# A decoder trunk on one core: picks of expert heads moved beside the next unit, and an inverse root that scales the last tanh

## The chip, the cores and the metric

One core of one Trainium2 chip. The metric is the device time of the whole program in microseconds (us), the median of three runs. Engines: TensorE (PE; PEld is its weight load), VectorE (DVE), ScalarE (ACT), GpSimd (POOL), SyncE (SP, which here only issues DMAs).

## The reference, cut to what matters

One inference step of a two-layer trunk for 256 prompt tokens and 64 sample tokens, width 1024, all float32. Layer 0: a Mamba-2 mixer, then a PEER channel mixer, then a per-layer embedding. Layer 1: dilated attention over shared keys and values (the samples also over 2048 cached ones), then PEER and embedding again. PEER and embedding:

```python
def peer(u, w_query, sub_keys, expert_u, expert_v):       # per token
    q = (u @ w_query).reshape(8 heads, 2, 128)
    s = einsum('thcd,ckd->thck', q, sub_keys)             # 128 scores, two per head
    top_s, top_i = top_k(s, 16)
    cand = top_s[..0.., :, None] + top_s[..1.., None, :]  # 16 x 16
    best_s, best_j = top_k(cand, 16)                      # 16 of 16384 experts per head
    gate = softmax(best_s)
    act = gelu(einsum('td,thkd->thk', u, expert_u[idx]))
    return einsum('thk,thkd->td', gate * act, expert_v[idx])

h = h + peer(rmsnorm(h, norm_ffn), ...)
g = sigmoid(rmsnorm(h, norm_ple) @ ple_w_gate)
h = h + (p @ ple_w_proj) * g
```

## The kernel before, in words

**Units and phases.** Tokens lie in three tiles t: two of 128 prompt tokens, one of 64 sample tokens. After the Mamba mixer (up to about 559 us) the work goes by six units (layer, tile): (0,0), (0,1), (0,2), (1,0), (1,1), (1,2). A unit needs 128 blocks of rows of expert_u and as many of expert_v (64 for tile 2). A block is one indirect DMA that POOL issues (line 2446): 128 rows of 4 KB, 0.52 MB. Phase ph mixes the "u" blocks of unit ph with the "v" blocks of unit ph-1 (`phase_blocks`, six u first). Rows go to a ring of 14 slots, in one order for all engines. DVE takes a u block: the dot with u (`dot`, line 2114), which frees the slot. PE takes a v block: the weighted sum into PSUM banks 6 and 7 (`combine`, line 1070), which frees its slot. POOL waits for the slot's last user, and at u blocks 0, 32, 64 and 96 for the pick of that quad (`expert`).

**What runs beside them.** Each engine's program holds a generator of steps beside the blocks (`beside(ph)`). `due(ph, i)` spreads its SIDE_STEPS evenly over the blocks of the phase. Phases 0 and 1 do the picks of layer 0. Phase 2 runs `chain(0)`, phase 3 `chain(1)`, phase 4 `chain(2)`, phases 5 and 6 the embedding of layer 1 for tiles 0 and 1. A chain has these steps: the embedding of layer 0 (11), keys and values (11), q (6 of 14), rotary embedding (`normalise_heads`), attention, output projection, a norm, and last `ask(t)`: the query projection of layer 1 (16 steps, 8 MB of weights), its scores, and the picks. `pick_quad` (DVE, 5 steps, from line 1967) finds for two heads, a quad of four score rows, the 16 best of 128 twice, then of 256, and the experts' numbers. For t = 0 and 1 `ask` has 29 steps; DVE waits 7, then picks four quads in 20 steps, then ends the softmax (`finish_select`, 2 steps). Phase 2 has 89 steps on 192 blocks, phase 3 has 96 on 192, phase 4 has 105 on 256.

**Scores.** ACT copies the scores of quad q to `sc[:, q % 2]` (`take_score`); for q of 2 and 3 it first waits for the pick of quad q-2.

**Between phases.** DVE ends the side steps, takes the sums of the unit before to h (`take_peer`) and copies the next u to PSUM (`show_u`, line 2137). From then on it can do dots of the new phase.

**SP.** Weights come through a ring of four slots of 1 MB (`load_weights`, line 267). In phase 3 SP loads the mask of the samples (line 1295, `masks[:, 768:2480]`) once the prompt's attention ends. In phase 4, when the q projections have ended, it issues the cached keys and values (lines 1283, 1285, 1287), and behind them the new heads' store (`store_heads`, line 1273). `sample_max(0)` on DVE (line 2249) waits for that store and for the masks.

**The tail.** After the last v block: `take_peer(1, 2)`, the norm of 64 rows x 1024 (square on ACT, 15 small DVE operations for the inverse root, scaling at line 1833), eight turns on PE, two copies on ACT, the gate's matmuls (line 1167), the projection (1173), tanh (1803), four DVE operations (2372, 2374, 2377), one store (1251).

Of the kernel before, what the change touches and what calls it, by code (L numbers as in the profile page):

```python
# [17 lines left out]
D = 1024  # L18
# [112 lines left out]
def build(nc, I, O, counts):  # L131
# [3 lines left out]
    with ctx:  # L135
# [236 lines left out]
        def chain_steps(t):  # L372
            return 5 + 6 + 5 + 6 + 14 + (14, 21, 38)[t] + 2 + 3 + 5 + (29, 29, 21)[t]
# [72 lines left out]
        angles = small[:, 1136:1184].rearrange("p (t c f) -> p t c f", t=3, c=2)  # L446

# [83 lines left out]
        def _(pe):  # L531
# [294 lines left out]
            def ask(t):  # L826
# [5 lines left out]
                for i in range(27 if t < 2 else 0):  # L832
# [298 lines left out]
            def beside(ph):  # L1131
# [5 lines left out]
                elif ph == 1:  # L1137
                    yield from second_select
                    yield from select(0, 2)
                elif ph < 5:  # L1140
                    yield from chain(ph - 2)
                else:
                    yield from embed(1, ph - 5)

# [15 lines left out]
            pe.wait_ge(*prow_in.at((1, 2)))  # L1160
            transposes(("pT", 1, 2), [(c * 128, p_rows[0:64, c * 128:(c + 1) * 128]) for c in range(2)])
            norm_transposes("ple1", (2,))
            pe.wait_ge(*freed(("pT", 1, 2)))
            gate = claim(pe, ("last_gate",))
            for k in range(KD):
# [4 lines left out]
            proj = claim(pe, ("last_proj",))  # L1170
            for k in range(2):
                for n in range(2):
                    mm = pe.matmul(proj[64 * n:64 * n + 64, :], pT[:, k, 0:64], proj_w[:, k, n * 512:(n + 1) * 512],
                                   start=(k == 0), stop=(k == 1))
            mm.then_inc(*full(("last_proj",)))
# [3 lines left out]
        def _(sp):  # L1179
# [68 lines left out]
            def store_tokens(t):  # L1248
                sp.wait_ge(*dve_done.at(("ple", 1, 1, t)))
                dst = O["y_prompt"][0, OFF[t]:OFF[t] + 128, :] if t < 2 else O["y_sample"].rearrange("b s d -> (b s) d")  # L1250
                sp.dma_start(dst, h[0:ROWS[t], t, :]).then_inc(stored.sem, 16)
# [39 lines left out]
            for t in range(3):  # L1291
                load_ple_rows(0, t, (0, t - 1) if t else None)
                if t == 2:
                    sp.wait_ge(*full_at(("oT", 1)))
                    sp.dma_start(masks[:, 768:768 + SCOLS], I["masks"][:, 1152:]).then_inc(*masks_in.mark("S", 16))
# [48 lines left out]
            sp.wait_ge(stored.sem, 144)  # L1344
# [6 lines left out]
        def _(act):  # L1351
# [81 lines left out]
            def take_score(l, t, q):  # L1433

                bank = filled(act, ("score", l, t, q))
                if q >= 2:
                    act.wait_ge(*dve_done.at(("gate_in", l, t, q - 2)))
                elif (l, t) != (0, 0):
                    l0, t0 = UNITS[3 * l + t - 1]
                    act.wait_ge(*dve_done.at(("gate_in", l0, t0, HPT[t0] // 2 - 1)))  # L1440
                freeing(act.activation(sc[:, q % 2, :, :], bank.rearrange("p (j r) -> p j r", j=4), ACT.Copy), ("score", l, t, q))  # L1441
# [94 lines left out]
            def ask(t):  # L1536
# [5 lines left out]
                for i in range(27 if t < 2 else 0):  # L1542
                    if 1 <= i <= 16:
                        take_query(t, i - 1)
                    if i in (6, 10, 14, 18):
                        take_score(1, t, (i - 6) // 4)
                    yield
# [221 lines left out]
            def beside(ph):  # L1769
# [5 lines left out]
                elif ph == 1:  # L1775
                    yield from second_select
                    yield from select(0, 2)
                elif ph < 5:
# [703 lines left out]
```

## Time and profile before

| | us |
|---|---|
| median of 3 runs | 2655.35 (2652.01 to 2661.92) |
| the profiled execution | 2655.78 |
| its span | 2653.9 |
| PE busy | 1841.1 (69%) |
| DVE busy | 1580.7 (60%) |
| POOL busy | 1329.1 (50%) |
| ACT busy | 301.0 (11%) |

The span runs from the first instruction to the last; the execution's own time has 1.9 us more around it. All rows come from this execution. L12 is line 12 of the kernel before; a name such as `arena<-peer_u` is what an instruction writes and reads. "Idle before" is the time in which the engine did nothing ahead of the instruction, and behind the arrow stands what ended it. A window (A:B, us from the span's start) gives its length, then busy us and the count of instructions for PE, PEld, DVE, ACT and POOL, then the granted TensorE clock (1.00 is full), the DMA engines' busy share and GB/s; where it is asked of one line, only the engines that run it are listed. A group of lines gives the count, busy us, mean ns of one, and idle us before it. A timeline gives start and length in us, the engine (SPq: SP's queue), line and instruction, and idle us in brackets.

### The profile page before, as it was taken

The numbers are of one execution on the slowest core, as the hardware profiler recorded it, in microseconds if no ns is written. First come the engines' busy times: TensorE is split into PE (matmuls) and PEld (weight loads), VectorE is DVE, ScalarE is ACT, GpSimd is POOL, SyncE is SP. The second block draws the span as 40 slices with busy tenths as digits, with TensorE's granted clock in tenths as the row PEclk, the third lists the DMA queues.
The fourth block names the chain that finished last, engine by engine and source line by source line (L and its number), as shares of the span: only waits on it lengthen the run. The fifth ranks groups of instructions, "written<-read, shape, count | busy, mean of one in ns | idle before, by whom it ended". The sixth has DMA issues, their size and how long they took to land. (4 is left out here: it accounts for less than half of the span.)

```text
span 2653.9 us, 23578 instructions
## 1 busy us (share of the span) xinstructions
PE 1841.1 (69%) x7672; PEld 817.0 (31%) x7672; DVE 1580.7 (60%) x3814; ACT 301.0 (11%) x698; POOL 1329.1 (50%) x1480
## 2 busy tenths in 40 slices
PE   7999789776605666678687667755765658566677
PEld 4477656632600010022342224431123422001112
DVE  2288854779798756652659739797454433833311
ACT  2133312100100000010110102100012100000000
POOL 0011432244646777754755446645554443577772
PEclk9999879887856665689888787876877868699999
DMA  4231227469999999999999999998999989999995
GB/s 149 96 127 64 85 88 235 148 252 382 401 339 345 409 409 409 409 399 384 390 403 405 352 371 362 405 402 302 397 395 348 335 316 381 386 409 409 409 408 231
DMA packets 325768, 859.13 MB, mean 324 GB/s; under 512 B 26825, under 2 KB 93337, under 8 KB 325617
## 3 DMA queue, kind: packets, MB, share of 16 engines
q0 software_dynamic: 184320, 671.17, 64.7%
q1 hardware_dynamic: 141326, 186.46, 20.3%
q8 instruction: 62, 1.02, 0.2%
q14 instruction: 60, 0.49, 0.1%
HBM read 845.25 MB, written 12.17 MB: 323 GB/s over the span
## 5 line engine op out<-in xcount | busy, mean ns | idle before, releaser
L2114 DVE SCALAR_TENSOR_TENSOR arena<-arena,banks 128x1024 f32<-128x1024 f32 x640 | 763.2, 1219 | 476.9 <-DMA arena<-peer_u,arena 471.1
L1070 PE MATMUL banks<-arena 128*32 128x512 f32 x2560 | 707.5, 727 | 340.2 <-DMA arena<-peer_v,arena 329.7
L2446 POOL DMA_INDIRECT arena<-peer_v,arena x640 | 610.3, 954 | 437.4 <-issue 202.4
L2446 POOL DMA_INDIRECT arena<-peer_u,arena x640 | 607.6, 949 | 418.6 <-issue 186.2
L1070 PEld LDWEIGHTS banks<-arena 128*32 128x32 f32 x2560 | 92.8, 117 | 829.8 <-DMA arena<-peer_v,arena 680.6
L863 PE MATMUL banks<-wring,uT 128*128 128x512 f32 (+3 forms) x448 | 224.2, 649 | 60.2 <-DMA wring<-w_q 31.5
L537 PE MATMUL banks<-cst,arena 128*128 128x128 f32 (+5 forms) x514 | 79.9, 305 | 182.7 <-DVE arena L2130 84.9
L863 PEld LDWEIGHTS banks<-wring,uT 128*128 128x128 f32 (+1 forms) x448 | 80.2, 189 | 210.1 <-issue 164.4
L606 PE MATMUL banks<-uT,wring 128*128 128x320 f32 x512 | 139.1, 433 | 0.0
L537 PEld LDWEIGHTS banks<-cst,arena 128*128 128x128 f32 (+5 forms) x514 | 63.1, 156 | 233.9 <-DVE arena L2130 86.7
L565 PE MATMUL banks<-wring,uT 128*128 128x512 f32 (+1 forms) x256 | 116.5, 612 | 0.0
L606 PEld LDWEIGHTS banks<-uT,wring 128*128 128x128 f32 x512 | 96.7, 190 | 40.2 <-issue 0.8
L2393 POOL COPY arena<-arena 128x3 f32<-128x3 f32 x32 | 6.0, 186 | 186.8 <-ACT arena L1407 186.8
L537 PE MATMUL banks<-cst,u 128*128 128x128 f32 (+1 forms) x244 | 40.3, 324 | 77.6 <-DVE u L1833 73.2
L807 PE MATMUL banks<-uT,wring 128*128 128x128 f32 x512 | 70.7, 297 | 14.1 <-issue 14.1
L1956 DVE MAX8 arena<-arena 128x8 f32<-128x128 f32 (+1 forms) x240 | 68.3, 326 | 16.7 <-ACT arena L1441 15.8
L807 PEld LDWEIGHTS banks<-uT,wring 128*128 128x128 f32 x512 | 65.2, 207 | 36.7 <-issue 36.7
L1959 DVE FIND_INDEX8 arena<-arena 128x8 uint32<-128x128 f32 (+1 forms) x240 | 76.1, 329 | 0.0
L1098 PE MATMUL banks<-wring,uT 128*64 128x512 f32 (+1 forms) x128 | 63.3, 649 | 13.0 <-DMA wring<-ssm_w_out 11.9
L2165 DVE TENSOR_SCALAR arena<-arena 128x512 f32<-128x512 f32 (+1 forms) x10 | 4.2, 425 | 111.4 <-ACT arena L1573 111.4
L2425 POOL TENSOR_TENSOR arena<-arena,small 128x1024 f32<-128x1024 f32 x10 | 19.3, 1930 | 96.9 <-PE banks L537 96.6
L565 PEld LDWEIGHTS banks<-wring,uT 128*128 128x128 f32 (+1 forms) x256 | 45.2, 182 | 69.0 <-issue 68.9
(249 smaller groups left out, 1988.6 us busy)
## 6 DMA issues: line engine op xcount, KB each, us to landing
wring<-peer_w_query SPq DMA_DIRECT2D x40, 1024.0 KB, 18.9
wring<-ssm_w_in SPq DMA_DIRECT2D x24, 1024.0 KB, 7.5
wring<-w_q SPq DMA_DIRECT2D x18, 1024.0 KB, 21.9
wring<-ssm_w_out SPq DMA_DIRECT2D x16, 1024.0 KB, 9.6
wring<-ple_w_gate SPq DMA_DIRECT2D x12, 1024.0 KB, 12.6
arena<-peer_u,arena POOLq DMA_INDIRECT x640, 11.7
arena<-peer_v,arena POOLq DMA_INDIRECT x640, 12.2
out_sample_ssm<-arena SPq DMA_DIRECT2D x16, 512.0 KB, 5.4
```

The lines of the kernel that those rows point to most:

```text
L537: mm = pe.transpose(bank[0:c, col:col + r], src, ident[0:r, 0:r])
L565: mm = pe.matmul(acc[t][0:ROWS[t], 0:w.shape[2]], uT[:, kk, OFF[t]:OFF[t] + ROWS[t]], w[:, k, :], start=(kk == 0), stop=(kk == kchunks - 1))
L606: mm = pe.matmul(acc[:, 0:NTOK], w[k // 4][:, k % 4, j * 128:(j + 1) * 128], uT[:, k, :], start=(k == 0), stop=(k == KD - 1))
L807: mm = pe.matmul(bank[:, 0:R], w[k // 4][:, k % 4, (b % 4) * 128:(b % 4 + 1) * 128], uT[:, k, OFF[t]:OFF[t] + R], start=(k == 0), stop=(k ...
L863: mm = pe.matmul(bank[0:ROWS[t], 0:w.shape[2]], uT[:, kk, OFF[t]:OFF[t] + ROWS[t]], w[:, k, :], start=(kk == 0), stop=(kk == kchunks - 1))
L1070: mm = pe.matmul(sums(t, at, half), place_of(t, at), rows_buf[:, k, half * 512:(half + 1) * 512], start=at < spots(t), stop=False, skip_gr ...
L1098: mm = pe.matmul(acc[t][0:ROWS[t], :], uT[:, kk, OFF[t]:OFF[t] + ROWS[t]], w[:, k, :], start=(kk == 0), stop=(kk == 15))
L1956: step(j, dve.max(out_v[:, o], values))
L1959: step(j, dve.max_index(out_i[:, o], out_v[:, o], values))
L2114: dve.scalar_tensor_tensor(rows_buf[:, k, :], rows_buf[:, k, :], 1.0, u_now, ALU.mult, ALU.mult, accum_out=pact[:, n % 2, at:at + 1]).then ...
L2425: s(pool.tensor_tensor(hh, hh, spread(ec[:, blk, :], 128), ALU.mult), pool_done, ("h0s", blk))
L2446: pool.indirect_dma_start(rows_buf[:, k, :], None, tables[kind], bass.IndirectOffsetOnAxis(ap=rows, axis=0))\
```

## The change

1. Of the second layer's picks for tiles 0 and 1, `ask(t)` keeps quad 0. Quads 1 to 3 and `finish_select` become `ask_rest(t)`, 17 steps, which runs in the next phase: `beside_half` takes one of its steps for every two of the chain. `ask` has 19 steps for 29.
2. Scores 2 and 3 of layer 1 go to a buffer of their own, `late_sc`, in the area of the masks.
3. The samples' mask lies over that buffer, so its load moves from phase 3 into phase 4, behind a wait for the pick of quad 3 of tile 1, and ahead of the cache loads.
4. The last tile: its sums stay in PSUM bank 6 (columns 0 to 511 in partitions 0 to 63, the others in 64 to 127). They are multiplied by the gain alone and turned; the inverse root is worked out beside the gate's matmuls and goes in as the scale of tanh. The projection is done six blocks before the end. `take_peer(1, 2)` goes. The rows are stored in two DMAs.

```diff
         def chain_steps(t):
-            return 5 + 6 + 5 + 6 + 14 + (14, 21, 38)[t] + 2 + 3 + 5 + (29, 29, 21)[t]
+            return 5 + 6 + 5 + 6 + 14 + (14, 21, 38)[t] + 2 + 3 + 5 + (19, 19, 21)[t]
...
+        late_sc = masks[:, 1152:2176].rearrange("p (q j k) -> p q j k", q=2, j=4)
+        def score_rows(l, q):
+            return (sc if l == 0 or q < 2 else late_sc)[:, q % 2]
...
+        last_u, last_h, last_gain = u[:, 2, 0:512], u[:, 2, 512:1024], u[:, 0, 512:1024]
+        LAST_PROJ_AT = BLOCKS[2] - 6
...
+        def beside_half(a, b):
+            for i, _ in enumerate(a):
+                if i % 2 == 0:
+                    next(b, None)
+                yield
+            for _ in b:
+                pass
...
                 # beside(ph), on PE, ACT and DVE
+                elif ph == 2:
+                    yield from chain(0)
                 elif ph < 5:
-                    yield from chain(ph - 2)
+                    yield from beside_half(chain(ph - 2), ask_rest(ph - 3))
...
             # PE; on ACT the same, with 19 for 27
-                for i in range(27 if t < 2 else 0):
+                for i in range(19 if t < 2 else 0):
...
+                if t == 2:
+                    yield from finish_select(1, t)
+
+            def ask_rest(t):
+                for _ in range(15):
                     yield
                 yield from finish_select(1, t)
...
+            def last_projection():
+                pe.wait_ge(*prow_in.at((1, 2)))
+                transposes(("pT", 1, 2), [(c * 128, p_rows[0:64, c * 128:(c + 1) * 128]) for c in range(2)])
+                pe.wait_ge(*freed(("pT", 1, 2)))
+                proj = claim(pe, ("last_proj",))
...
+                    if ph == 6 and at == LAST_PROJ_AT:
+                        last_projection()
...
-            norm_transposes("ple1", (2,))
+            pe.wait_ge(*dve_done.at("last_u"))
+            for m in range(2):
+                transposes(("last_hT", m), [(j * 128, last_u[:, (2 * m + j) * 128:(2 * m + j + 1) * 128]) for j in range(2)])
             gate = claim(pe, ("last_gate",))
-            for k in range(KD):
+            for at, k in enumerate((0, 4, 1, 5, 2, 6, 3, 7)):
+                if at % 4 == 0:
+                    pe.wait_ge(*freed(("last_hT", at // 4)))
...
             # SP, store_tokens
+                    for n in range(2):
+                        sp.dma_start(O["y_sample"].rearrange("b s d -> (b s) d")[:, n * 512:(n + 1) * 512],
+                                     last_h[64 * n:64 * n + 64, :]).then_inc(stored.sem, 16)
...
             # SP, from before the loads of chain(2) to behind its q projections
                 if t == 2:
                     for n in range(3):
                         sp.wait_ge(*full_at((f"wq{t}", n, t)))
+                    sp.wait_ge(*full_at(("oT", 1)))
+                    sp.wait_ge(*dve_done.at(("gate_in", 1, 1, 3)))
+                    sp.dma_start(masks[:, 768:768 + SCOLS], I["masks"][:, 1152:]).then_inc(*masks_in.mark("S", 16))
                     load_cache(0, 0, (1,))
...
             # ACT, take_score
-                if q >= 2:
+                if q >= 2 and l == 0:
                     act.wait_ge(*dve_done.at(("gate_in", l, t, q - 2)))
+                elif q >= 2:
+                    if t > 0:
+                        act.wait_ge(*dve_done.at(("gate_in", 1, t - 1, q)))
...
             # ACT, the tail
+            for m in range(2):
+                bank = filled(act, ("last_hT", m))
+                freeing(act.activation(turned[:, 2 * m:2 * m + 2], ...), ("last_hT", m))
+            act.wait_ge(*dve_done.at("last_u"))
+            s(act.activation(u[:, 0, 0:512], sum_banks[0], ACT.Square, accum_out=last_ssq), act_done, "last_ssq")
+            s(act.activation(last_h, sum_banks[0], ACT.Copy), act_done, "last_h")
             bank = filled(act, ("last_gate",))
+            act.wait_ge(*dve_done.at("last_rstd"))
-            freeing(act.activation(sgate, bank, ACT.Tanh, scale=0.5), ("last_gate",))
+            freeing(act.activation(sgate, bank, ACT.Tanh, scale=last_rstd), ("last_gate",))
...
             # DVE
             def ask(t):
                 for _ in range(7 if t < 2 else 9):
                     yield
-                for q in range(HPT[t] // 2):
+                if t < 2:
+                    yield from pick_quad(1, t, 0)
+                    for _ in range(7):
+                        yield
+                else:
+                    for q in range(2):
+                        yield from pick_quad(1, t, q)
+                    yield from finish_select(1, t)
+
+            def ask_rest(t):
+                for q in (1, 2, 3):
                     yield from pick_quad(1, t, q)
                 yield from finish_select(1, t)
...
             # DVE, the tail; the copy of the gain to last_gain stands ahead of phase 6
-            norm("ple1", PLE_SLOT, (2,), "ple12")
+            dve.wait_ge(*sums_closed.at((1, 2)))
+            s(dve.tensor_tensor(last_u, sum_banks[0], last_gain, ALU.mult), dve_done, "last_u")
+            dve.wait_ge(*act_done.at("last_ssq"))
...
+            rsqrt(last_rstd, last_ssq, last_tmp)
+            s(dve.tensor_scalar(last_rstd, last_rstd, 0.5, None, ALU.mult), dve_done, "last_rstd")
             dve.wait_ge(*freed(("last_gate",)))
-            s(dve.tensor_scalar(sgate, sgate, 0.5, 0.5, ALU.mult, ALU.add))
             bank = filled(dve, ("last_proj",))
-            freeing(dve.tensor_tensor(sgate, sgate, bank, ALU.mult), ("last_proj",))
-            for n in range(2):
-                hh = h[0:64, 2, n * 512:(n + 1) * 512]
-                s(dve.tensor_tensor(hh, hh, sgate[64 * n:64 * n + 64, :], ALU.add), dve_done, ("ple", 1, n, 2))
+            freeing(dve.scalar_tensor_tensor(sgate, sgate, 1.0, bank, ALU.add, ALU.mult), ("last_proj",))
+            dve.wait_ge(*act_done.at("last_h"))
+            s(dve.scalar_tensor_tensor(last_h, sgate, 0.5, last_h, ALU.mult, ALU.add), dve_done, ("ple", 1, 1, 2))
```

## Rows read from the trace of the kernel before

**Rows 1.** The first line of the profile's page

```profile
span 2653.9 us, 23578 instructions
```

**Rows 2.** Windows of phases 2, 3 and 4, in that order

```profile
1116.20:1442.40 326.20, 246.02 (x1115) 103.13 (x1115) 173.69 (x463) 37.10 (x86) 184.59 (x192) 0.87 1.02 396
1442.40:1786.90 344.50, 234.47 (x955) 115.94 (x957) 256.19 (x631) 42.69 (x91) 183.80 (x193) 0.80 0.99 379
1786.90:2278.90 492.00, 304.67 (x1345) 113.41 (x1345) 253.45 (x587) 59.84 (x128) 244.18 (x256) 0.76 0.96 356
```

**Rows 3.** Windows: a stretch of gathers alone, and four others

```profile
959.00:1099.00 140.00, 93.64 (x250) 12.06 (x248) 92.32 (x227) 1.89 (x5) 105.64 (x112) 0.63 1.03 409
1439.00:1499.00 60.00, 38.00 (x110) 11.06 (x107) 47.77 (x136) 4.78 (x12) 29.52 (x31) 0.80 0.93 352
1579.00:1619.00 40.00, 19.65 (x79) 9.79 (x79) 31.46 (x61) 4.77 (x9) 19.16 (x20) 0.70 0.80 282
1779.00:1839.00 60.00, 26.41 (x82) 5.41 (x79) 57.13 (x155) 3.55 (x10) 28.71 (x30) 0.55 0.83 294
1999.00:2039.00 40.00, 24.41 (x155) 14.87 (x155) 16.33 (x27) 8.56 (x15) 15.24 (x17) 0.73 0.97 323
```

**Rows 4.** Windows over three picks: all engines, then line 2114 on DVE alone

```profile
1372.90:1439.40 66.50, 49.54 (x284) 26.67 (x280) 56.80 (x208) 4.99 (x15) 33.62 (x34) 0.85 1.03 402
1372.90:1439.40 66.50, 12.29 (x20) 0.85 1.03 402
```

**Rows 5.** Timeline of DVE, line 2137: start, length, instruction

```profile
1134.82 1.23 DVE L2137 COPY banks<-u 128x1024 f32<-128x1024 f32 x1
1466.95 1.23 DVE L2137 COPY banks<-u 128x1024 f32<-128x1024 f32 x1
1817.29 1.23 DVE L2137 COPY banks<-u 128x1024 f32<-128x1024 f32 x1
```

**Rows 6.** Windows from line 2137 to the rotary's end, phases 3 and 4

```profile
1466.90:1605.70 138.80, 84.77 (x229) 32.42 (x229) 81.20 (x165) 12.88 (x23) 65.82 (x68) 0.79 0.93 347
1817.30:1966.40 149.10, 98.96 (x304) 24.49 (x304) 80.36 (x160) 11.68 (x24) 80.85 (x84) 0.79 1.00 380
```

**Rows 7.** Groups of DVE's lines in those windows, the first in phase 3, the second in 4

```profile
L2305 DVE TENSOR_REDUCE small<-arena 128x24 f32<-128x1536 f32 x1 | 1.8, 1752 | 18.8 <-ACT arena L1684 18.8
L2114 DVE SCALAR_TENSOR_TENSOR arena<-arena,banks 128x1024 f32<-128x1024 f32 x45 | 53.5, 1219 | 46.2 <-DMA arena<-peer_u,arena 45.8
```

**Rows 8.** Timeline, SP and DVE in phase 4; and one DMA issue: KB, us to landing

```profile
1944.22 0.37 SPq L1283 DMA_DIRECT2D wring<-cache_k  x1
2010.10 0.58 SPq L1273 DMA_DIRECT2D out_sample_v<-arena  x1
2013.75 2.52 DVE L2249 TENSOR_TENSOR arena<-banks,uT 128x512 f32<-128x512 f32 x4 [25.50 <-issue]
uT<-masks SPq DMA_DIRECT2D x1, 856.0 KB, 24.1
```

**Rows 9.** Timeline of the tail; then windows of line 1167 on PE and PEld

```profile
2627.36 1.07 PE L1082 MATMUL banks<-h,cst 64*64 64x512 f32 x4
2637.21 9.39 PE L1167 MATMUL banks<-arena,uT 128*64 128x512 f32 x32 [0.58 <-ACT uT L1362]
2646.42 1.90 PE L1173 MATMUL banks<-arena 128*64 128x512 f32 x8
2646.69 0.60 ACT L1803 ACTIVATE arena<-banks 128x512 f32<-128x512 f32 x1 [9.58 <-PE banks L1167]
2648.43 0.69 DVE L2374 TENSOR_TENSOR arena<-arena,banks 128x512 f32<-128x512 f32 x1 [0.61 <-PE banks L1173]
2650.58 0.51 SPq L1251 DMA_DIRECT2D out_y_sample<-h  x1
2637.20:2642.00 4.80, 4.79 (x12) 1.66 (x14) 0.51 0.02 3
2642.00:2646.40 4.40, 4.40 (x22) 1.41 (x18) 1.00 0.00 0
```

More of the change, by code:

```diff
@@ L446, in build @@
         angles = small[:, 1136:1184].rearrange("p (t c f) -> p t c f", t=3, c=2)
+        last_u, last_h, last_gain = u[:, 2, 0:512], u[:, 2, 512:1024], u[:, 0, 512:1024]
+        last_ssq, last_tmp, last_rstd = (small[:, 1184 + i:1185 + i] for i in range(3))
+        LAST_PROJ_AT = BLOCKS[2] - 6
         PLE_SLOT, KV_SLOT, MIX_SLOT, FFN_SLOT = 0, 1, 0, 1
@@ L1139, in beside @@
                     yield from select(0, 2)
+                elif ph == 2:
+                    yield from chain(0)
                 elif ph < 5:
-                    yield from chain(ph - 2)
+                    yield from beside_half(chain(ph - 2), ask_rest(ph - 3))
                 else:
                     yield from embed(1, ph - 5)
+            def last_projection():
[3 more added lines that the diff above has]
+                proj = claim(pe, ("last_proj",))
+                for k in range(2):
+                    for n in range(2):
+                        mm = pe.matmul(proj[64 * n:64 * n + 64, :], pT[:, k, 0:64], proj_w[:, k, n * 512:(n + 1) * 512],
+                                       start=(k == 0), stop=(k == 1))
+                mm.then_inc(*full(("last_proj",)))
             open_bank = [None]
@@ L1169, in _ @@
             mm.then_inc(*full(("last_gate",)))
-            proj = claim(pe, ("last_proj",))
-            for k in range(2):
-                for n in range(2):
-                    mm = pe.matmul(proj[64 * n:64 * n + 64, :], pT[:, k, 0:64], proj_w[:, k, n * 512:(n + 1) * 512],
-                                   start=(k == 0), stop=(k == 1))
-            mm.then_inc(*full(("last_proj",)))
         @block.sync
@@ L1249, in store_tokens @@
                 sp.wait_ge(*dve_done.at(("ple", 1, 1, t)))
-                dst = O["y_prompt"][0, OFF[t]:OFF[t] + 128, :] if t < 2 else O["y_sample"].rearrange("b s d -> (b s) d")
-                sp.dma_start(dst, h[0:ROWS[t], t, :]).then_inc(stored.sem, 16)
+                if t < 2:
+                    sp.dma_start(O["y_prompt"][0, OFF[t]:OFF[t] + 128, :], h[:, t, :]).then_inc(stored.sem, 16)
+                else:
+                    for n in range(2):
+                        sp.dma_start(O["y_sample"].rearrange("b s d -> (b s) d")[:, n * 512:(n + 1) * 512],
+                                     last_h[64 * n:64 * n + 64, :]).then_inc(stored.sem, 16)
             sp.wait_ge(*freed(("yT", 2, 3)))
@@ L1343, in _ @@
             store_tokens(2)
-            sp.wait_ge(stored.sem, 144)
+            sp.wait_ge(stored.sem, 160)
             sp.wait_ge(*newst_out.at("all"))
@@ L1541, in ask @@
                     yield from ask_rows()
-                for i in range(27 if t < 2 else 0):
+                for i in range(19 if t < 2 else 0):
                     if 1 <= i <= 16:
@@ L1546, in ask @@
                         take_score(1, t, (i - 6) // 4)
+                    yield
+                if t == 2:
+                    yield from finish_select(1, t)
+            def ask_rest(t):
+                for _ in range(15):
                     yield
@@ L1777, in beside @@
                     yield from select(0, 2)
+                elif ph == 2:
+                    yield from chain(0)
                 elif ph < 5:
-                    yield from chain(ph - 2)
+                    yield from beside_half(chain(ph - 2), ask_rest(ph - 3))
                 else:
@@ L1787, in _ @@
                         tanh_of(n)
+                    if ph == 6 and at == LAST_PROJ_AT:
+                        bank = filled(act, ("pT", 1, 2))
+                        freeing(act.activation(pT[:, :, 0:64], bank[:, 0:256].rearrange("p (c r) -> p c r", c=2)[:, :, 0:64],
+                                               ACT.Copy), ("pT", 1, 2))
                     if kind == "v" and at % BATCH == 3 and BATCH < at < BLOCKS[UNITS[n][1]] - BATCH:
@@ L1971, in pick_quad @@
                 for c in (0, 2):
-                    top16(*((sc[:, q % 2, i, :], top_v[:, i, :], top_i[:, i, :]) for i in (c, c + 1)))
+                    top16(*((score_rows(l, q)[:, i, :], top_v[:, i, :], top_i[:, i, :]) for i in (c, c + 1)))
                     yield
@@ L2105, in ask, with ask_rest @@
                     yield
-                for q in range(HPT[t] // 2):
+                if t < 2:
+                    yield from pick_quad(1, t, 0)
+                    for _ in range(7):
+                        yield
+                else:
+                    for q in range(2):
+                        yield from pick_quad(1, t, q)
+                    yield from finish_select(1, t)
+            def ask_rest(t):
+                for q in (1, 2, 3):
                     yield from pick_quad(1, t, q)
@@ L2350, in beside @@
                     yield from select(0, 2)
+                elif ph == 2:
+                    yield from chain(0)
                 elif ph < 5:
-                    yield from chain(ph - 2)
+                    yield from beside_half(chain(ph - 2), ask_rest(ph - 3))
                 else:
@@ L2360, in _ @@
                     show_u(ph)
+                else:
+                    dve.wait_ge(*gain_in[PLE_SLOT].at("ple10"))
+                    for n in range(2):
+                        rows = slice(64 * n, 64 * n + 64)
+                        s(dve.tensor_copy(last_gain[rows, :], gain[rows, PLE_SLOT, n * 512:(n + 1) * 512]))
                 for i, (kind, n, at) in enumerate(phase_blocks(ph)):
```

22 lines of the change are left out of this document (8 added, 14 removed).

## The prediction

> **What bounds the kernel now.** I began with the span [rows 1], then the stretches: phases 2, 3 and 4 issue 192, 192 and 256 gathers of expert rows (the POOL column; 193 counts one that straddles the edge) in 326, 345 and 492 us [rows 2]. In a stretch with gathers alone the DMA engines move 409 GB/s and POOL issues 112 in 140 us, 1.25 us each [rows 3]. At that pace the three phases would take 240, 240 and 320 us. The rest is mostly weights and caches on the same 16 DMA engines, and the phases' mean rates, 396, 379 and 356 GB/s, are near 409 [rows 2]. So the resource that sets the time is the DMA, and what an edit can give back is only **the time in which it is not full**: of a stretch's length, 1 - rate/409. That is 8.4 us around the start of phase 3, 12.4 us around 1600, 16.9 us around the start of phase 4 and 8.4 us around 2020 [rows 3].
>
> The cause at the starts is VectorE (DVE). Around the start of phase 4 it is busy 57.1 of 60 us [rows 3], because at the end of phases 2 and 3 it picks all four quads of the next unit between the dots of gathered rows. A quad: from 1372.9 to 1439.4 three are picked, DVE is busy 56.80 us, of which 12.29 are dots, so 14.8 us each [rows 4]. Late dots free their row slots late, and DVE opens the next phase (its copy of u, line 2137) 24.6 us after POOL began phase 3 and 30.4 us after it began phase 4, but 18.6 us at phase 2, whose picks had been spread [rows 2, 5].
>
> **The change, part by part.**
> Quads 1 to 3 leave the ends of phases 2 and 3. 44 us of DVE work leave each end. As the DMA was full there (weights took the room), I don't count 44 us but what the starts lost: DVE opens phase 3 earlier by 24.6 - 18.6 = 6 us and phase 4 by 30.4 - 18.6 = 12 us. Bounds: 0, if other work makes the starts late, and 8.4 + 16.9 = 25 us, all that the DMA lost there. Taken: **-18**.
>
> They arrive in the first 34 steps of the chains of phases 3 and 4, up to the rotary embedding. There DVE was busy 81.2 of 138.8 us and 80.4 of 149.1 us [rows 6]. Three quads and the softmax's end add 3 x 14.8 + some 3 = 47 us (an estimate from rows 4): 128 of 139 and 127 of 149. It fits, if DVE fills time in which it waited. In phase 4 46.2 us of idle were waits for rows, which late dots don't pay; in phase 3 18.8 us were one wait for ScalarE's squares of q [rows 7], and this goes too, if DVE comes there later than they. DVE over 92% busy will make PE wait for some norms. Bounds: -12 (the loss around 1600 goes) to +11 + 10 (in each stretch DVE keeps 20 to 30 us of idle). Taken: **+3 and +2**.
>
> The chains of phases 2 and 3 have 10 steps fewer (79 for 89, 86 for 96) over the same blocks, so weights are asked for less fast, and PE waits a little less for those of q and of the query. Between 0 and -6; taken **-2**. Scores 2 and 3 of the second layer get a buffer of their own in the masks' area, so ScalarE no longer waits there for a pick; PE and ScalarE copies are the same in number: 0. The picks' new places come before POOL needs them: quad 1 ends by block 22 of a phase, POOL asks at block 45 less 14 slots. 0.
>
> The new wait is on SP. The sample masks (856 KB) move from phase 3 behind the last q weights of phase 4 and a wait for quad 3's pick, ahead of the cached keys and values. Queued behind it: the cache loads, from 1944.22, and the store of the new heads, at 2010.10, which DVE awaits at 2013.75 after 25.5 us of idle [rows 8]. Quad 3's pick is due at chain step 28, the last q weight's matmuls at 27, so SP waits one step (5 us) or more; the masks add their issue and their bytes, 24.1 us to landing at worst in a full queue [rows 8], 2.1 us at 409 GB/s. A start 14 us later doesn't cost 14: gathers stand still during that stall, and the loads then flow alone. Bounds: +1 (wait and issue hidden) to +20. Taken: **+4**, near the low end, because the DMA lost only 8.4 us in the whole old stall.
>
> The tail. Before, from the sums' last matmul (begins 2627.36, 1.07 us) to the store's issue at 2650.58 it took 22.2 us [rows 9]: two copies, square, inverse root (15 small operations), scaling, eight turns, gate matmuls 9.39 us, projection, tanh, four DVE operations. Now the sums are multiplied by the gain (one 128x512 DVE operation, 0.69 us like the multiplication at line 2374 [rows 9]), turned in four 128x128 pieces and copied in halves (1.4 us to the first half, an estimate; 1.0 to 2.0 by operations like line 1803's 0.60), then the gate; the inverse root runs beside it: ready at about 7 us after the sums, before the gate ends. After it tanh 0.60 and two DVE operations of 0.70. The gate's 32 passes: 12 took 4.80 us at a granted clock of 0.51 and 22 took 4.40 us at 1.00, so 0.40 and 0.20 us each [rows 9], the levels of 1.2 and 2.4 GHz. The clock had fallen while PE idled through the norm; now it idles under 2 us, so I take 32 x 0.20 = 6.4 us (at worst 32 x 0.40 = 12.8). Sum: 0.2 + 0.7 + 1.4 + 6.5 + 0.7 + 1.5 = 11.0 us for 22.2: -11.2. PE gets two turns and the projection (1.90 us at line 1173, [rows 9]) at block 58 of the last phase, five rows before the last; it waits for rows there at times: between 0 and +2.8, taken +1. The sample rows leave in two stores, a second issue of 0.5 us [rows 9]: +0.5. Taken **-10**, bounds -11 and -4.
>
> The Trainium skill, "DMA: Bandwidth & Descriptors", section "Rules for kernel authors", speaks against that last part: two transfers to disjoint partition halves serialise, and one transfer should be used. By it the halves gain nothing and the sum is as above; if they ran side by side, it would be under 0.5 us better. No row before shows such a pair.
>
> Sum: -18 + 5 - 2 + 4 - 10 = **-21**. The profiled execution took 2655.8 us (1.9 outside its span), the median is 2655.35, the same within 0.5. Forecast: **2635 us**.
>
> **The rivals.** 0.5% (13.3 us) is about what a measurement of this kernel can tell from no change: limits 2642 and 2669.
> (A) *The picks only change places.* DMA and DVE are both nearly full, so what the starts give back, the first steps take. For: 128 of 139 us. Against: DVE's 46 us of waits for rows in phase 4. The tail alone is left, with the SP wait: 2655 - 10 + 4 = 2649, or 2642 to 2660.
> (B) *The queue evens out fully.* All 25 us at the starts, 12 us around 1600 and 6 us in phase 2 come back, SP costs nothing: 2655 - 43 - 10 = 2602; halfway, 2620.
> (C) *DVE becomes the bound in the first 34 steps* and ends slower. Price: each us of idle that DVE keeps beyond 11 us in phase 3 and 22 in phase 4 lengthens the stretch. Idle before was 57.6 and 68.7. To pass 2669 it must cost 13 more than the rest gains, 13 + 10 + 18 + 2 - 4 = 39 us: the two must keep 72 of 126 us. At 86 kept: 2683. Against: 46 us of the second were waits for rows [rows 7].
> (D) *The change does not do what it says at the end*: the clock stays at 1.2 GHz and the root is late; tail -4 for -10, total 2641. Included in the forecast's edge.
>
> **Numbers.** Forecast (2625 to 2642, with D) 0.41; B (below 2625) 0.21; A 0.30; C 0.08. The range leaves out the far ends of B and C: 2612 to 2658. Faster by over 0.5% is the forecast and B, 0.62; A is the same, 0.30; slower 0.08. The forecast's own range is 2625 to 2642.
>
> **What the profile would show.** Right: DVE opens phases 3 and 4 18 to 20 us after POOL begins them; the 60 us around them run near 400 GB/s; DVE about 127 us busy from there to the rotary; one gap of 25 to 35 us before the first sample mask addition; 11 to 12 us from the sums to the store's issue, gate at a granted clock of 1.0. Wrong: DVE without idle in those stretches and PE waiting for u or the indices (C, A); SP asking for the cache over 20 us after the last q matmuls.

## The result and the profile after

The changed kernel takes 2614.64 us (median of 4 runs, 2610.68 to 2618.01), the kernel before 2655.73 us in its 4 runs beside them: ratio 0.9842, 95% interval 0.9818 to 0.9867. That is 41 us less; the forecast was 2635 us, from a sum of -21. The profiled execution took 2618.01 us, 37.8 less than the one of before.

The first line of the changed kernel's page; its span is 37.7 us shorter [rows 1]:

```profile
span 2616.2 us, 23576 instructions
```

Windows of phases 2, 3 and 4, which answer to [rows 2]:

```profile
1109.90:1422.80 312.90, 234.85 (x1039) 96.14 (x1039) 144.80 (x340) 35.33 (x82) 183.31 (x193) 0.88 1.02 397
1422.80:1752.20 329.40, 234.04 (x958) 114.84 (x959) 258.65 (x635) 42.14 (x89) 183.02 (x193) 0.80 1.01 391
1752.20:2250.40 498.20, 308.81 (x1419) 121.35 (x1419) 279.37 (x705) 62.15 (x134) 243.91 (x256) 0.80 0.97 366
```

DVE's copy of u at the start of phases 2, 3 and 4 ([rows 5] of before):

```profile
1128.55 1.23 DVE L2205 COPY banks<-u 128x1024 f32<-128x1024 f32 x1
1447.90 1.23 DVE L2205 COPY banks<-u 128x1024 f32<-128x1024 f32 x1
1776.03 1.23 DVE L2205 COPY banks<-u 128x1024 f32<-128x1024 f32 x1
```

Phases 2 and 3 are 13.3 and 15.1 us shorter, phase 4 is 6.2 longer. To say where the time went, one ledger between marks that both kernels have; the loss is the length times (1 - rate/409), as in the prediction:

| stretch | before, us | after, us | rate, GB/s | loss, us |
|---|---|---|---|---|
| start to the first gather of an expert row | 558.9 | 552.4 | | |
| to DVE's copy of u, phase 2 | 575.9 | 576.1 | 387, 387 | 31.0, 31.0 |
| to the same in phase 3 | 332.1 | 319.3 | 396, 396 | 10.6, 10.2 |
| to the end of the rotary embedding | 138.7 | 151.6 | 348, 381 | 20.7, 10.4 |
| to the copy of u, phase 4 | 211.7 | 176.5 | 382, 400 | 14.0, 3.9 |
| to the end of the rotary embedding | 149.1 | 161.9 | 380, 394 | 10.6, 5.9 |
| to the first sample mask addition | 47.3 | 44.7 | 362, 356 | 5.4, 5.8 |
| to the copy of u, phase 5 | 290.4 | 294.0 | 356, 353 | 37.6, 40.3 |
| to the sums' last matmul | 324.2 | 323.2 | 400, 400 | 7.1, 7.1 |
| to the store's issue | 22.1 | 13.0 | | |
| to the end | 3.3 | 3.4 | | |

From the first gather to the sums the time fell by 22 us and the loss by 22.5 (137.0 to 114.5). Both kernels move the same bytes there, so the two must agree: the ledger says where the time went, not why. The 6.5 us ahead of the first gather lie in code that nobody touched (last section).

The largest piece is the start of phase 4, which lies across one of the marks (14.0 to 3.9 ahead of it, 10.6 to 5.9 behind it). POOL begins phase 4 at 1786.90 before. While DVE picked, up to there, the DMA was full. Around DVE's copy of u it was not. Windows of before: the last 65 us of phase 3, then 20 us to either side of the copy; behind them the same 40 us after:

```profile
1722.00:1787.00 65.00, 37.70 (x198) 23.02 (x200) 63.31 (x208) 4.01 (x11) 27.47 (x29) 0.75 1.03 401
1797.00:1837.00 40.00, 15.48 (x52) 4.23 (x52) 37.84 (x94) 3.55 (x10) 18.93 (x21) 0.55 0.75 247
```

```profile
1756.00:1796.00 40.00, 21.39 (x99) 8.71 (x96) 27.76 (x84) 4.53 (x13) 17.88 (x20) 0.79 1.03 406
```

In the first window 29 gathers and 7.8 MB of loads by SP filled the queue, and a gather took 22 us to land; in the second there were gathers alone, landing in 5 to 6 us. What POOL and SP waited for meanwhile (us in total, times, longest), from 1757 to 1840 before and from 1760 to 1800 after:

```profile
SPq L267 <- PE banks L882: 76.8, 1, 76.8
POOL arena L2446 <- DVE arena L2114: 33.6, 18, 4.5
```

```profile
SPq L267 <- PE banks L906: 32.7, 1, 32.7
POOL arena L2526 <- DVE arena L2182: 9.1, 7, 3.0
```

L2114 and L2182 are the dot, L267 the load of weights. Both waits go back to DVE: POOL stands behind late dots, and SP behind PE's first matmuls of phase 4's chain (L882), which come behind DVE's norm (line 1833, at 1827.17). So late DVE work held up the gathers and the weights at once, and it cost time here when the loads asked for earlier had run out. No run separates the two waits.

The start of phase 3 fills up as well. Two 60 us windows after, which lie at the starts as the second and fourth of [rows 3] do before; the two had lost 25.3 us, and now lose 1.8:

```profile
1420.00:1480.00 60.00, 40.49 (x178) 17.09 (x179) 34.62 (x110) 7.05 (x18) 28.64 (x31) 0.86 1.03 404
1744.00:1804.00 60.00, 40.75 (x205) 19.54 (x203) 43.35 (x121) 6.09 (x17) 32.26 (x35) 0.86 1.03 402
```

### The profile page after: what moved, and what is told of

The parts are those of the page before. It is cut to its first block, busy times and chain, and to the rows that moved or that the text cites. A ratio compares the mean times of both kernels' runs of the same rounds, so it can differ in the third digit from the quotient of the medians.

```text
span 2616.2 us, 23576 instructions
## 1 busy us (share of the span) xinstructions
PE 1826.9 (70%) x7668; PEld 812.8 (31%) x7668; DVE 1578.3 (60%) x3815; ACT 301.2 (12%) x699; POOL 1324.7 (51%) x1480
## 4 chain that ended last, share of the span: by engine, by line
DMA 25%; POOL 15%; PE 13%; issue 7%; DVE 6%; SPq 3%; ACT 0%; POOLq 0%; DVEq 0%; ACTq 0%
POOL arena L2526 15%; DMA arena<-peer_v,arena 12%; PE banks L887 5%; DMA wring<-w_q 5%; PE banks L1094 3%; DMA arena<-peer_u,arena 3%; DVE arena L2182 2%; DMA wring<-cache_v 2%; SPq L1326 2%; DMA wring<-w_kv 1%; PE banks L1003 1%; SPq L1324 1%; DMA wring<-peer_w_query 1%; PE banks L825 1%; PE banks L555 1%
## 5 line engine op out<-in xcount | busy, mean ns | idle before, releaser
L2182 DVE SCALAR_TENSOR_TENSOR arena<-arena,banks 128x1024 f32<-128x1024 f32 x640 | 763.5, 1219 | 463.5 <-DMA arena<-peer_u,arena 457.3
L2014 DVE MAX8 arena<-arena 128x8 f32<-128x128 f32 (+1 forms) x208 | 60.7, 333 | 18.4 <-ACT arena L1483 17.5
L2017 DVE FIND_INDEX8 arena<-arena 128x8 uint32<-128x128 f32 (+1 forms) x208 | 67.4, 336 | 0.0
L2505 POOL TENSOR_TENSOR arena<-arena,small 128x1024 f32<-128x1024 f32 x10 | 19.1, 1909 | 92.9 <-PE banks L555 92.6
L1003 PE MATMUL banks<-wring,arena 128*64 128x128 f32 x208 | 27.8, 298 | 41.8 <-DMA wring<-cache_v 41.7
```

The source lines that it names most:

```text
L1003: pe.matmul(bank[rows, 0:128], pts[:, b, rows], cache[:, 1, 13 * b2 + b, :], start=(b == 0), stop=False)
L2014: step(j, dve.max(out_v[:, o], values))
L2017: step(j, dve.max_index(out_i[:, o], out_v[:, o], values))
L2182: dve.scalar_tensor_tensor(rows_buf[:, k, :], rows_buf[:, k, :], 1.0, u_now, ALU.mult, ALU.mult, accum_out=pact[:, n % 2, at:at + 1]).then ...
```

## Experiments

Medians, and ratios against runs of the kernel before that stand beside them on the same chip (medians 2653.4 to 2655.5 us). e9 to e11 ran on another chip than e1 to e8. Medians of different rows are compared below as they are; where the ratios say something else, that is given. In the diffs "-" is the changed kernel, with e7 in its place for e9.

| kernel | us | ratio, 95% |
|---|---|---|
| e1_tail_only | 2643.68 | 0.9951, 0.9934 to 0.9968 |
| e2_picks_only | 2626.69 | 0.9892, 0.9876 to 0.9909 |
| e3_half | 2623.77 | 0.9885, 0.9868 to 0.9901 |
| e4_again (the changed kernel) | 2616.82 | 0.9846, 0.9825 to 0.9867 |
| e5_t0_only | 2639.35 | 0.9948, 0.9929 to 0.9967 |
| e6_t1_only | 2620.54 | 0.9880, 0.9859 to 0.9901 |
| e7_pace | 2622.85 | 0.9895, 0.9873 to 0.9918 |
| e8_order | 2612.56 | 0.9859, 0.9830 to 0.9888 |
| e9_load_end | 2639.76 | 0.9932, 0.9908 to 0.9955 |
| e10_load_start | 2644.83 | 0.9955, 0.9939 to 0.9971 |
| e11_warm | 2620.39 | 0.9856, 0.9827 to 0.9884 |

**The two parts alone.** e1 takes back all that concerns the picks, e2 all that concerns the tail, e4 is the changed kernel once more.

```diff
 e1: in chain_steps, ask, beside, take_score and SP
-            ... + (19, 19, 21)[t]
+            ... + (29, 29, 21)[t]
-                    yield from beside_half(chain(ph - 2), ask_rest(ph - 3))
+                    yield from chain(ph - 2)
 e2: after the last block
-            pe.wait_ge(*dve_done.at("last_u"))
+            norm_transposes("ple1", (2,))
```

> The kernel before with the new tail alone (picks, their steps and the mask load as before). If the parts add up as the two traces say (from the last sums to the store's issue 22.2 us before, 13.0 after), it is 9 to 11 us faster: about 2645. If part of the 41 us is something that both parts share, or that lies ahead of the first gather, it is 15 us or more faster: under 2640.

> The changed kernel with the tail of before. Theory 1, what counts is the time in which the DMA was not full: about 25 us come back at the two starts and around the rotary, none is given to the first steps: 22 to 28 us faster, 2627 to 2634, and with the tail's 10 about 34 in all. Theory 2, my sum: 11 us faster, 2644. If the median's 41 us are all of the change, 31 us faster: 2625.

> The changed kernel once more, beside the others on one chip. If the 6.5 us by which its first gather was early (552.4 for 558.9) are the state of TensorE's clock in that one execution, the first gather is anywhere from 552 to 560 here and in the other kernels, and the gain against before is 30 to 42. If they belong to the change, it is at 552 to 554 here and in the kernel with the picks alone or the tail alone, and at 559 in no changed kernel.

The tail gives 10 us (2654.0 to 2643.7), the picks 27 to 29 (2654.0 to 2626.7 in e2; 2643.7 to 2616.8 or 2614.6 with the tail in). The parts add up. The tail's term was right and all that was missing is in the picks, forecast at 11.

**How many quads move, and of which tile.** e3 leaves quads 0 and 1 at the end of the phase; e5 moves tile 0's quads alone (end of phase 2 to phase 3), e6 tile 1's (end of phase 3 to phase 4).

```diff
 e3: DVE, ask (24 steps)
                     yield from pick_quad(1, t, 0)
+                    yield from pick_quad(1, t, 1)
 e5
-                if t < 2:
+                if t in (0,):
 e6
-                if t < 2:
+                if t in (1,):
```

> The changed kernel, but quads 0 and 1 stay at the end of phases 2 and 3 and only 2 and 3 move (24 steps in ask for 19). Theory 1: DVE has room for one more quad at the end (57 us of dots and one pick beside 65 us), so the starts hardly get later: within 5 us of the changed kernel. Rival, each quad at the end costs its DVE time: 2 x 14.8 us at the ends, less what the first steps get back: 10 to 15 us slower than the changed kernel.

> The changed kernel, but only tile 0's quads 1 to 3 move (end of phase 2 to phase 3); tile 1 picks all four at the end of phase 3 as before. Theory 1, the DMA's idle time is what counts: 8 us come back at the start of phase 3 and 2 around the rotary: 8 to 11 us, with the tail's 10 about 2635. Rival, the marks on DVE count: phase 2 is 13 to 15 us shorter to the copy of u, the stretch to the rotary 11 longer, so 3 us, with the tail 2641.

> The changed kernel, but only tile 1's quads 1 to 3 move (end of phase 3 to phase 4). Theory 1: 16 us come back at the start of phase 4, with the tail about 2628. Rival by the marks: phase 3 is 36 us shorter, the stretch to the rotary 14 longer, 3 less to the first sample mask addition: 25 us, with the tail 2619.

Against e1, tile 0's move gives 4 us and tile 1's 23; together 27. By the ratios it is 1 and 19, each with some 7 us either way, so tile 0's part can't be told from nothing. The expectations that counted the DMA's idle time (2635 and 2628) missed both; those by the marks (2641 and 2619) came within 2 us. Both moves shorten their chain by 10 steps and both take 44 us of DVE work from an end, so neither alone explains the difference. In e5 the stretch at the end of phase 3 keeps its 212.1 us, in e6 it has 178.3.

The DMA's rate in the 20 us to either side of DVE's copy of u of phase 4 tells the kernels apart: 247, 245, 241, 246 and 222 GB/s in before, e1, e5, e9 and e10, which have all the DVE work at the end of phase 3, and 394 to 406 in the eight others. e3, with one quad more at the end than the changed kernel, has 394: it keeps all but some 7 us (10 by the ratios), between its two expectations.

**Chain length.** e7 moves the picks but leaves ten empty steps in both chains:

```diff
-            ... + (19, 19, 21)[t]
+            ... + (29, 29, 21)[t]
                     yield from pick_quad(1, t, 0)
-                    for _ in range(7):
+                    for _ in range(17):
                         yield
```

> The changed kernel with ten empty steps at the end of the chains of phases 2 and 3 (89 and 96 steps again), the picks moved. If slower asking for weights gives 2 us (my term), it is 2 us slower, within 1% of noise the same. If the shorter chains give a large part of the gain (the steps before the query come later and the weights meet fewer gathers), it is 8 us or more slower.

2622.85 us: the shorter chains are worth 6 to 8 us by the medians and 13 to 14 by the ratios, not 2. Between the two expectations (2, and 8 or more) this doesn't decide. From the rotary embedding to the copy of u of phase 4 it took 191.7 us, with the short chain 176.5; but the stretch ahead is 10 us shorter in e7 (141.3 for 151.6), and the opening of phase 3 comes 3 us later (322.3 for 319.3), so the net is what the medians say.

**Work at the end, work at the start.** e9 is e7 with 42 us of DVE work put back at the end of phase 3, with the picks themselves in phase 4. e10 is e1 with the same 42 us beside the first steps of phase 4. The added results are used by nobody.

```diff
 e9: DVE, ask; e10: the same 15 steps through beside_half in phase 4
+            def spare_work():
+                for _ in range(4):
+                    s(dve.tensor_tensor(onehot, best_a..., cst[:, C_IOTA:C_IOTA + 16]..., ALU.is_equal))
...
-                    for _ in range(17):
+                    for i in range(17):
+                        if t == 1 and i < 15:
+                            spare_work()
                         yield
```

> The kernel of e7_pace (picks moved, ten steps of the chains left empty; 2622.85 us), with 60 more VectorE operations of 0.69 us (the pick's own comparison of 128x512, results unused) in the 15 empty steps at the end of phase 3, where tile 1's quads 1 to 3 used to be picked: 42 us of VectorE work in their old place, while the picks themselves stay in phase 4. Theory (the gain of tile 1's move is the removal of VectorE work from the end of phase 3, whatever the work is): the stretch from the rotary embedding of phase 3 to the opening of phase 4 goes from 192 back to 205 to 215 us, the stretch behind it gives little back, and the kernel takes 2635 to 2645 us. Rival (VectorE had room there; the gain is that the picks are ready in another order or that the buffers of the scores are free earlier): the stretch stays within 4 us of 192 and the kernel within 5 us of 2623.

> The kernel with the tail alone changed (2643.68 us; all picks at their old places), with the same 60 VectorE operations of 0.69 us (42 us) beside the first 30 steps of phase 4: the price of the arrivals alone, without what the removal gives. My prediction's term was +2 us, so 2646. Theory formed from the marks: VectorE reaches the rotary embedding of phase 4 5 to 13 us later (158 to 165 to 170 us), but the bytes that the DMA moves meanwhile shorten what follows, so that the whole costs 0 to 6 us: 2644 to 2650. Rival (the arrivals cost what the marks show, and the move gained more than it seems): over 2653.

This is the decisive pair. e9 takes 2639.76 us, 17 more than e7 (10 by the ratios, with 1 to 18 as the interval; no run of either lies among those of the other). The stretch from the rotary embedding to the copy of u in e7, as a window, and then POOL's wait for the dots in it (us in total, times, longest):

```profile
1599.80:1791.50 191.70, 148.98 (x702) 86.52 (x702) 139.11 (x293) 29.41 (x66) 117.55 (x124) 0.76 1.03 401
```

```profile
POOL arena L2526 <- DVE arena L2182: 8.5, 11, 2.1
```

and in e9 (its dot is L2189):

```profile
1598.60:1805.60 207.00, 139.58 (x705) 78.69 (x706) 179.57 (x355) 29.43 (x66) 121.54 (x124) 0.81 1.00 384
```

```profile
POOL arena L2533 <- DVE arena L2189: 40.3, 38, 2.9
```

DVE 139 to 180 us busy, the rate 401 to 384 GB/s, the wait for dots 8.5 to 40.3 us, 15.3 us more time. The picks are in their new place in both, so it is DVE's load there that costs, whatever its kind. The 20 us to either side of the copy of u, in e7 and then in e9, account for 15 us of DMA time:

```profile
1771.00:1811.00 40.00, 22.77 (x65) 4.20 (x62) 30.42 (x86) 3.24 (x9) 21.41 (x23) 0.57 1.01 397
```

```profile
1785.00:1825.00 40.00, 12.08 (x46) 3.34 (x45) 37.98 (x97) 3.25 (x9) 19.91 (x20) 0.60 0.73 246
```

e10 against e1 (2644.83 to 2643.68, good to some 6 us): the same load at the start of phase 4 costs 1 us. From the copy of u to the rotary embedding in e1, the same two views:

```profile
1813.70:1971.40 157.70, 100.77 (x304) 25.74 (x304) 80.56 (x160) 11.68 (x24) 80.86 (x84) 0.77 0.98 368
```

```profile
POOL arena L2495 <- DVE arena L2153: 5.4, 3, 3.2
```

and in e10:

```profile
1817.90:1975.90 158.00, 95.94 (x304) 25.15 (x304) 120.96 (x220) 11.68 (x24) 84.64 (x84) 0.78 0.98 367
```

```profile
POOL arena L2505 <- DVE arena L2153: 13.7, 8, 3.6
```

40 us more of DVE work there, and the stretch has the same length and rate; it was expected 5 to 13 us longer. So one load is worth 17 us in one place and 1 in the other. The arrivals in phase 3 have no such run of their own. From e1 the whole can be walked: tile 0's quads moved and ten steps left in (to e9) -4, the load gone from the end of phase 3 (to e7) -17, shorter chains (to the changed kernel) -6 to -8: -27 to -29. These are differences of medians, each good to some 6 to 9 us.

**The order on SP.** e8 puts the new heads' store ahead of the second keys of the cache.

```diff
                     load_cache(0, 1)
-                    load_cache(1, 0)
                 store_heads(t)
...
+                    load_cache(1, 0)
```

> The changed kernel, but SP issues the new heads' store and the four moves of new values ahead of the loads of the second pair's cached keys. Theory: DVE's 26 us of waiting in phase 4 are the store's place in SP's queue, 19 us behind the end of the values' loads, so DVE adds the first mask about 18 us earlier. In time, by the DMA's idle time there (some 7 to 10 us), 4 to 8 us faster. Rival: the keys then come late and the next wait takes the place: within 3 us of the changed kernel.

The first sample mask addition in the changed kernel and then in e8, from DVE's timeline:

```profile
1982.65 2.52 DVE L2317 TENSOR_TENSOR arena<-banks,uT 128x512 f32<-128x512 f32 x4 [26.24 <-issue]
```

```profile
1965.22 2.52 DVE L2317 TENSOR_TENSOR arena<-banks,uT 128x512 f32<-128x512 f32 x4 [12.23 <-issue]
```

14 us of idle are gone and the addition stands 31.0 us behind the rotary embedding for 44.7, but the stretch behind it takes 307.7 us for 294.0. The wait moved on to the keys: PE stands 22.9 us behind their load. The expected 4 to 8 us did not come (by the ratios e8 is 3 us slower): 2612.56 us can't be told from 2614.64 and 2616.82, so no version here clearly beats the changed kernel.

**The clock in the tail.** e11 puts two more matmuls (results overwritten) between the sums and the turns:

```diff
+            gate = claim(pe, ("last_gate",))
+            for _ in range(2):
+                pe.matmul(gate[0:64, :], ident[:, 0:64], gate_w[:, 0, 0:512], start=True, stop=True)
             pe.wait_ge(*dve_done.at("last_u"))
```

> The changed kernel with two more TensorE matmuls of 64x512 (results overwritten) between the sums' last matmul and the wait for VectorE's multiplication by the gain, so that TensorE idles less ahead of the turns. In both profiles of the changed kernel the granted clock fell to 0.5 for 3 to 4 us in the gate's matmuls (8.75 us, sums to store 13.0). Theory (the fall comes from TensorE's idling of 0.9 and 0.4 us just before): the gate runs at 1.00, 6.5 to 7.0 us, and sums to store takes 11.3 to 11.8 us: 1 to 2 us faster, 2613 to 2616. Rival (the fall doesn't depend on those gaps, since it did not come in other versions with the same tail): the gate takes 8.7 us again, or the two matmuls cost their own 0.4 us and nothing else changes: 2616 to 2618.

Timeline of the tail of the changed kernel, which answers to [rows 9]:

```profile
2598.78 1.07 PE L1106 MATMUL banks<-h,cst 64*64 64x512 f32 x4
2599.97 0.69 DVE L2446 TENSOR_TENSOR u<-banks,u 128x512 f32<-128x512 f32 x1 [5.20 <-PE banks L1106]
2600.72 0.66 PE L555 MATMUL banks<-cst,u 128*128 128x128 f32 x4 [0.86 <-DVE u L2446]
2601.25 0.80 ACT L1853 ACTIVATE uT<-banks 128x256 f32<-128x256 f32 x2 [8.46 <-PE banks L555]
2601.78 8.75 PE L1208 MATMUL banks<-arena,uT 128*64 128x512 f32 x32 [0.41 <-ACT uT L1853]
2606.12 0.15 DVE L2452 TENSOR_SCALAR small<-small 128x1 f32<-128x1 f32 x1
2610.62 0.69 ACT L1861 ACTIVATE arena<-banks,small 128x512 f32<-128x512 f32 x1 [7.22 <-PE banks L1208]
2611.40 0.69 DVE L2455 SCALAR_TENSOR_TENSOR arena<-arena,banks 128x512 f32<-128x512 f32 x1 [5.12 <-ACT arena L1861]
2612.12 0.69 DVE L2457 SCALAR_TENSOR_TENSOR u<-arena,u 128x512 f32<-128x512 f32 x1
2612.84 1.15 SPq L1289 DMA_DIRECT2D out_y_sample<-u  x2
```

Its gate matmuls in two windows: 12 passes at a granted clock of 0.59, 22 at 1.00, as in [rows 9] of before:

```profile
2601.70:2605.90 4.20, 4.12 (x12) 1.43 (x14) 0.59 0.01 4
2605.90:2610.40 4.50, 4.50 (x22) 1.40 (x18) 1.00 0.00 0
```

The turns and the gate of the same tail in e1:

```profile
2631.88 0.66 PE L555 MATMUL banks<-cst,u 128*128 128x128 f32 x4 [0.86 <-DVE u L2415]
2632.94 7.09 PE L1200 MATMUL banks<-arena,uT 128*64 128x512 f32 x32 [0.41 <-ACT uT L1834]
```

and the added matmuls and the gate in e11:

```profile
2606.89 1.93 PE L1202 MATMUL banks<-arena,cst 128*64 128x512 f32 x4
2609.72 7.09 PE L1210 MATMUL banks<-arena,uT 128*64 128x512 f32 x32 [0.32 <-ACT uT L1855]
```

In e11 the gate took 7.09 us, but the two matmuls put the turns 0.9 us later, so sums to store took 12.2 us for 13.0, and the median shows nothing (2620.39). It doesn't settle the cause: e1 has the gaps of the changed kernel, 0.86 and 0.41 us, and a gate of 7.09 us too. The clock fell in the profiles of the changed kernel, e4, e9 and e10, and in those of e1, e3, e5, e6, e7 and e8 it did not. What decides stays open; it is worth 1.7 us. The expected 2613 to 2616 us did not come.

## Why the prediction was wrong in size

Right: what bounds these phases is the DMA, the picks' gain is time in which it isn't full, and that time lies at the starts, which now run at 404 and 402 GB/s, as the prediction's signs had it. Right too are the sign, and the tail: 13.0 us from sums to store in this profile and 11.3 in others, for 11.0 plus the second store's 0.5; -9 to -11 for -10. The root's last operation began at 2606.12 (L2452), 4.5 us ahead of tanh, and from the store's issue to the end it is 3.4 us with two stores and 3.3 with one. The Trainium skill, "DMA: Bandwidth & Descriptors", section "Rules for kernel authors", has it that two transfers to disjoint partition halves serialise and that one should be used; no run here shows in which order the two moved, and splitting them cost nothing that can be seen.

**The step that failed** is the sum of the picks' terms, -18 + 5 - 2 + 4 = -11, where the runs show -27 to -29: above all the -18, which was sized by DVE's lag and not by what the DMA lost, and the +9 charged for the arrivals and SP's wait. The mechanism held; the sizes erred, nearly all to the same side.

| term | taken, us | what the runs and windows show |
|---|---|---|
| the starts | -18 | 25.3 us of loss became 1.8; the load at the end of phase 3 alone is 17 us (e7 to e9; 10 by the ratios) |
| the arrivals | +3, +2 | +1 in phase 4, good to some 6 us (e10); none measured alone in phase 3 |
| the chains' pace | -2 | -6 to -8 (e7; more by the ratios) |
| SP's wait and the masks | +4 | none to be seen; no run has it alone |

These overlap, and don't add up to the us. The first term went wrong where the prediction left its own rows. It had read what the DMA lost at the starts, 8.4 and 16.9 us, and took that as the bound; for the size it took instead how far DVE's opening lags behind POOL's, 6 and 12 us. The lag was no measure: it should have fallen to 18 to 20 us, and stands at 25.1 in phase 3 (24.6 before) and 23.8 in phase 4 (30.4), while the loss went nearly whole. "As the DMA was full there (weights took the room), I don't count 44 us" held: 401 GB/s up to the edge, and 42 us of such work there are worth 17 (e7 to e9). Moving tile 0's quads is worth 4 (e1 to e5), not clear of nothing.

The second part is the +9 for the work's new places. From e1 to e9 the whole move is in except the relief at the end of phase 3 and the shorter chains; the sum has -6 + 9 = +3 for that, the medians -4.

The arrivals: by the marks they look like 13 us each (138.7 to 151.6, 149.1 to 161.9), and DVE is busy 133.7 and 125.7 us for my 128 and 127. But the marks are DVE's, not the DMA's. Windows between them, after:

```profile
1447.90:1599.50 151.60, 91.96 (x241) 32.95 (x241) 133.72 (x369) 13.19 (x24) 74.92 (x77) 0.76 0.99 381
1776.00:1937.90 161.90, 99.86 (x305) 24.87 (x305) 125.69 (x354) 11.98 (x25) 81.25 (x84) 0.82 1.03 394
```

Against [rows 6] 77 gathers lie in the first for 68, at 381 GB/s for 347: the stretch is longer and holds more of the phase's bytes (57.8 MB for 48.3), and the next pays that back. And yet POOL stood 45.6 us behind dots in the first of them, for 19.1 before, as much as in the 211.7 us at the end of phase 3 before (43.7). Its waits behind PE fell there from 42.2 to 19.6 us, and the rate rose: a wait of the issuer is not yet a price. The wait for ScalarE's squares shrank from 18.8 to 9.8 us, as argued.

The pace, -2: 6 to 8 measured by the medians (e7), at or beyond the far end of its bounds, 0 to -6.

SP's wait and the masks, +4 with bounds +1 to +20: nothing to be seen. The masks were issued at 1914.38 and landed in 6.3 us, not 24.1. SP's timeline, after, and the group of that DMA issue:

```profile
1914.38 0.34 SPq L1351 DMA_DIRECT2D uT<-masks  x1
...
1930.20 10.66 SPq L1326 DMA_DIRECT2D wring<-cache_v  x1
...
1978.57 0.60 SPq L1312 DMA_DIRECT2D out_sample_v<-arena  x1
```

```profile
uT<-masks SPq DMA_DIRECT2D x1, 856.0 KB, 6.3
```

DVE's idle ahead of the mask addition is 26.24 us for 25.50: one gap, as named. From the rotary embedding there it took 2.6 us less than before. The stretch behind it took 294.0 us for 290.4, but 294.0 in e1 too, where the masks stay in phase 3.

Of the rivals, A (2649) fell with e2, C with the result: the idle that DVE keeps is 18 and 36 us, past the 11 and 22 from which C was to cost, and e10 shows no price for it in phase 4. D happened half, in some executions (1.7 us). B, halfway (2620), was nearest, and by its mechanism: nearly all that the starts lost came back, and SP's wait cost nothing that can be seen. How much came back around 1600 and in phase 2 can't be read from single executions: e1's loss by the same ledger is 144.1 where before's is 137.0 with the same picks, and from the copy of u of phase 4 to the rotary embedding it took 157.7 us for 149.1 in the same code.

## What to carry to other kernels

Where the DMA bounds a kernel, read its rate in short windows across each edge, and price a change by what is lost there: here 401 GB/s up to the edge and 247 around the opening behind it. A mean over a phase hides that, and the lag of another engine didn't measure it. Then ask for that place what the engines that issue the transfers wait for (here POOL's and SP's waits, by releaser). Their waits cost nothing while other transfers filled the queue, and cost time when these had run out: 42 us of DVE work cost 17 us at one place and 1 at another, and POOL stood 45.6 us behind dots in phase 3's first stretch at no price that a run shows. A mark on one engine that moves later isn't a price as long as the queue moves more bytes meanwhile.

## What the hardware showed beside that

- The first gather, in code that is the same in all, came between 552.0 and 561.1 us over the thirteen profiles (before, after and the eleven runs). In the window from 350 to 445 us the granted clock was 0.85 before and 0.92 after, with 18 and 23 instructions on POOL, none of them a gather; before, then after:

```profile
350.00:445.00 95.00, 83.31 (x392) 55.32 (x390) 41.38 (x84) 15.86 (x36) 18.21 (x18) 0.85 0.49 159
```

```profile
350.00:445.00 95.00, 82.86 (x424) 56.63 (x424) 43.59 (x87) 16.13 (x35) 22.49 (x23) 0.92 0.54 179
```

The latest, 561.1, is e7's, a changed kernel, so the early gather isn't the change's doing. A single pair of profiles is good to this much, and 6.5 of the pair's 37.7 us are this. Whether the clock made it isn't shown.

- The same load of 856 KB took 24.1 us to land in a full queue [rows 8] and 6.3 us behind the q projections; of the fifteen loads of the cache that SP issues next, seven held its queue for 5.3 to 10.7 us apiece and the others for under 2.4.
